# Weight slots 8256 bytes apart and moving rows at four byte offsets, in a two-layer decoder trunk

## The reference

```python
for i in range(DEPTH):                       # DEPTH = 2
    g = norm_gains[i]
    y = swiglu(rms_norm(h, g[0]), ffn_w_gate[i, 0], ffn_w_up[i, 0], ffn_w_down[i, 0])
    h = h + 0.5 * rms_norm(y, g[1])
    u = rms_norm(h, g[2])
    y = mixer_ab(u, ...) if i % 2 == 0 else mixer_cd(u, ...)
    h = h + rms_norm(y, g[3])
    y = swiglu(rms_norm(h, g[4]), ffn_w_gate[i, 1], ffn_w_up[i, 1], ffn_w_down[i, 1])
    h = h + 0.5 * rms_norm(y, g[5])
return h[:, N_META:]

def swiglu(x, w_gate, w_up, w_down):         # 1024 -> 2816 -> 1024
    return (jax.nn.silu(x @ w_gate) * (x @ w_up)) @ w_down
```

## Time and profile before

| what | value |
|---|---|
| median of the runs shown | 1092.51 us (1092.21 to 1092.80) |
| the profiled execution | 1092.85 us, span 1091.1 us |
| granted TensorE clock, mean | 0.998 |
| busy: TensorE, VectorE, ScalarE | 1077.3, 703.8, 545.5 us |
| DMA engines, mean | 54.1% on the weight queue |

### The profile page before, as it was taken

The page is one execution under the profiler, slowest core; times in us unless marked ns, Lnnn a source line. Parts: engine busy times, 40 slices in busy tenths (PEclk is TensorE's granted clock), DMA queues, the critical chain, the costliest instruction groups (busy, mean ns, idle before and its releaser), DMA issues.

```text
span 1091.1 us, 19370 instructions
## 1 busy us (share of the span) xinstructions
PE 1077.3 (99%) x8599; PEld 1046.3 (96%) x8599; DVE 703.8 (65%) x770; ACT 545.5 (50%) x635; POOL 1.6 (0%) x13
## 2 busy tenths in 40 slices
PE   9999999999999999999999999999999999999997
PEld 8999999999999999999999999999999899999986
DVE  6856654588996777655546755654568867665552
ACT  5644343467564765343544644343475766444431
POOL 0000000000000000000000000000000000000000
PEclk9999999999999999999999999999999999999999
DMA  9666556857751545564554655555553244666451
GB/s 315 194 193 184 179 174 167 163 112 182 156 163 39 155 155 171 177 192 148 178 180 127 219 180 168 183 173 178 162 179 117 78 155 156 192 193 206 143 173 39
DMA packets 173072, 180.02 MB, mean 165 GB/s; under 512 B 7508, under 2 KB 165804, under 8 KB 172988
## 3 DMA queue, kind: packets, MB, share of 16 engines
q1 hardware_dynamic: 172668, 177.66, 54.1%
q10 hardware_dynamic: 320, 1.11, 0.3%
HBM read 177.05 MB, written 1.71 MB: 164 GB/s over the span
## 4 chain that ended last, share of the span: by engine, by line
PE 88%; DVE 7%; ACT 2%; DMA 2%; issue 1%; SPq 0%; ACTq 0%; DVEq 0%
PE ps L1800 23%; PE ps L1801 23%; PE ps L1802 23%; PE ps L1905 5%; PE ps L1890 2%; PE ps L1889 2%; PE ps L1888 2%; PE ps L2030 2%; PE ps L1872 2%; PE ps L1834 1%; PE ps L1837 1%; PE ps L1838 1%; DVE w_lo L1179 1%; DVE hT L1228 1%; DMA a_dram<-dN 1%
## 5 line engine op out<-in xcount | busy, mean ns | idle before, releaser
L1800 PE MATMUL ps<-u,w_hi 128*128 128x272 f32 (+1 forms) x1648 | 473.6, 287 | 2.1 <-DVE w_lo L1179 1.8
L1801 PE MATMUL ps<-u,w_hi 128*128 128x272 f32 (+1 forms) x1648 | 470.0, 285 | 0.0
L1802 PE MATMUL ps<-u,w_lo 128*128 128x272 f32 (+1 forms) x1648 | 469.7, 285 | 0.0
L1179 DVE TENSOR_TENSOR w_lo<-raw,w_hi 128x2048 fp32r<-128x2048 f32 (+2 forms) x167 | 369.5, 2236 | 106.0 <-ACT w_hi L717 106.0
L717 ACT ACTIVATE w_hi<-raw 128x2048 fp32r<-128x2048 f32 (+2 forms) x167 | 310.8, 1871 | 162.2 <-PE ps L1802 140.0
L1800 PEld LDWEIGHTS ps<-u,w_hi 128*128 128x128 f32 x1648 | 310.4, 188 | 4.2 <-ACT yT L846 1.4
L1801 PEld LDWEIGHTS ps<-u,w_hi 128*128 128x128 f32 x1648 | 310.4, 188 | 0.3
L1802 PEld LDWEIGHTS ps<-u,w_lo 128*128 128x128 f32 x1648 | 310.1, 188 | 0.0
L1800 PE MATMUL ps<-hid,w_hi 128*128 128x272 f32 x528 | 151.3, 286 | 0.0
L1801 PE MATMUL ps<-hid,w_hi 128*128 128x272 f32 x528 | 151.3, 286 | 0.0
L1802 PE MATMUL ps<-hid,w_lo 128*128 128x272 f32 x528 | 151.3, 286 | 0.0
(11 more groups left out here) (345 smaller groups left out, 1045.2 us busy)
## 6 DMA issues: line engine op xcount, KB each, us to landing
raw<-ffn_w_up SPq DMA_DIRECT2D x44, 1024.0 KB, 5.4
raw<-ffn_w_gate SPq DMA_DIRECT2D x43, 1024.0 KB, 5.3
raw<-ffn_w_down SPq DMA_DIRECT2D x24, 896.0 KB, 4.9
raw<-ffn_w_down SPq DMA_DIRECT2D x20, 1024.0 KB, 5.1
raw<-ab_w_in SPq DMA_DIRECT2D x16, 1024.0 KB, 14.6
raw<-cd_w_in SPq DMA_DIRECT2D x9, 1024.0 KB, 5.5
raw<-ab_w_out SPq DMA_DIRECT2D x4, 1024.0 KB, 7.0
raw<-cd_w_out SPq DMA_DIRECT2D x4, 1024.0 KB, 5.1
```

The source lines that it names most:

```text
L1179: dve.tensor_tensor(dst, src, w_hi[:, n % NW, 0:rows(n) * CB].bitcast(F32), ALU.subtract)\
L1800: pe.matmul(o, wh, rhs_hi[:, kk, tok], start=first and kk == 0, stop=False)
L1801: pe.matmul(o, wh, rhs_lo[:, kk, tok], start=False, stop=False)
L1802: ins = pe.matmul(o, wl, rhs_hi[:, kk, tok], start=False, stop=last and kk == rows(n) - 1)
```

## The change

The slots of raw, w_lo and w_hi get 16 floats more and so lie 8256 bytes apart. The place of u_room and of hidden becomes 0 modulo 256 instead of 64, and the shifts of the sublayers get four values. gains moves from the spare floats of the rows to a place of its own, and lnv from a place of its own to a part of the scratch memory. No instruction is added, removed or moved on any engine; the operands' addresses change.

```diff
@@ -48,9 +48,10 @@
 BANK = 512
 ROW = 320
 SPARE = 288
-PLACE = 64
-U_AT = (0, 0, 0, 0, 0, 64)
-HID_AT = (0, 0, 0, 64)
+PLACE = 0
+SLOT = RAW + 16
+U_AT = (0, 64, 128, 192, 64, 192)
+HID_AT = (64, 192, 0, 0)
@@ -172,11 +173,13 @@
         ring = place[0]
-        raw = sb("raw", [NR, RAW])
-        w_lo = at("w_lo", [P, NR, RAW], F32R, ring)
-        w_hi = sb("w_hi", [NW, RAW], F32R)
+        raw = sb("raw", [NR, SLOT])
+        w_lo = at("w_lo", [P, NR, SLOT], F32R, ring)
+        w_hi = sb("w_hi", [NW, SLOT], F32R)
         ss = sb("ss", [T])
         rstd = sb("rstd", [2, T])
+        gains = sb("gains", [3, 4 * KD])
+        place[0] += (PLACE - place[0]) % 256
         u_place = place[0]
@@ -191,10 +194,9 @@
-        lnv = sb("lnv", [T])
         ident = sb("ident", [P])
         ones = sb("ones", [P])
-        w_ba, gains = spare[:, 0:KD, :], spare[:, KD:KD + 3, :]
+        w_ba = spare[:, 0:KD, :]
@@ -207,6 +209,7 @@
         y_sq = at("y_sq", [P, 2, 2, T], F32, scratch)
+        lnv = at("lnv", [P, T], F32, scratch + (HG + 1) * TP * 4)
@@ -1728,7 +1731,7 @@
-            dve.tensor_copy(gains, ps[:, 0, 0:12 * KD].rearrange("p (r c) -> p r c", c=32)).then_inc(s_gains, 1)
+            dve.tensor_copy(gains[:, :, :], ps[:, 0, 0:12 * KD].rearrange("p (r c) -> p r c", c=32)).then_inc(s_gains, 1)
```

## The result

The changed kernel took 1105.16 us, the median of 1103.45 and 1106.87, against 1092.51: ratio 1.011, 95% interval 1.0082 to 1.0138. It is slower by 12.7 us. The forecast was 1106.5.

A forecast was written before the change was run, and what follows sets the result against it. TensorE was taken as the bound, its matmul spacing set by byte distances. Terms 12.7 + 1.2 - 0.2 + 0.9 + 0.3 - 0.8 = +14.1 us on the 1092.51 median gave 1106.5 us; range 1097 to 1113, main case's own 1103 to 1112.

The forecast's parts named there:

- What bounds the kernel: Whole kernel: TensorE, busy 1077.3 of 1091.1 us, is the bound; its waits for w_lo should stay under 3 us.
- The distance decides, not the place: TensorE matmuls: the moving row's byte distance from the weights, not its own address, sets the time between matmul starts.
- Even distances slow, odd ones fast: 272-column matmuls: distances 0 or 128 modulo 256 take 127.5 ns, distances 64 or 192 take 123.3 ns.
- The price: 272-column matmuls in FFNs, mixers and output projection: half of 6048 get 4.2 ns slower, +12.7 us.
- The last FFN: Input matmuls of the last sublayer's FFN, 256 columns: 528 get 2.2 ns slower, +1.2 us.
- The last down projection: Last sublayer, weights streaming 512 columns: half of 264 matmuls go from 233.3 to 240 ns, +0.9 us.
- Cover in the mixers: Mixer sublayers: a third of 2.5 us of slower matmuls hides behind VectorE and ScalarE work, -0.8 us.
- Passings between blocks: TensorE between weight blocks: some 65 passings from slow to fast rows cost a few ns each, +0.3 us.
- rival 5: Half of the blocks: w_hi and w_lo 128 apart change distance twice per matmul triple, +12 us, 1118.5 us; chance 0.07.
- rival 4: Half of the blocks: weights away from 128 shed part of the extra 10 ns, 118.3 ns, 1077.5 us; chance 0.06.
- rival 3: All matmuls: addresses don't matter in the long run, time stays 1092.5 us; chance 0.08.
- rival 2: All matmuls: only an even weight start together with an even moving-row start is slow, 1099.5 us; chance 0.12.

## Why the prediction was right

Forecast 1106.5, measured 1105.16, inside the range 1097 to 1113 and inside the case's own 1103 to 1112. By stages the sum of 14.1 us stands against 10.5 in the profiled execution: the three FFNs cost 1 us more than forecast, the mixers and the last sublayer 4.2 less. That the total lands 1.3 us off is in part luck. By its steps:

- *What bounds the kernel*: right. TensorE's busy time grew by 11.7 us and the span by 10.5; the other engines' busy times and the landing stayed, and the waits for w_lo fell from 1.8 to 0.8 us, under the 3 us that the prediction set as its sign.
- *The distance decides, not the place*: right, shown by shifting everything (ratio 0.9996) and by equal distances at different places in the changed kernel (blocks 9 and 92).
- *Even distances slow, odd ones fast*: wrong. Distance 192 is slow, 126.7 ns, shown by the kernel with that distance throughout. The step failed because I took the odd row 192 in the earlier trace rows for a steady state: its three matmuls stand between two slow rows and their sum, 0.37 us, is not what 24 of them do. The stretch with 256 columns at 192 was steady, but 256 columns follow another table (117.8 at 192, 120.0 at 0), and I carried it over.
- *The price*: 4.2 ns for half of 6048 against 2.1, 3.3 and 3.3 ns for three quarters; 2.1 and 2.2 ns on the mean. Two errors, a class missed and a price too high, cancelled; that is luck. With one distance per sublayer the same step would have been far off: it gives 0 for distance 192, where the run had 3.3 ns a matmul.
- *The last FFN*: +1.2 forecast, -0.1 measured. Its blocks have 120.0 ns at worst, but block 147, for one, has 113.3 for its 48 matmuls, with w_hi at distance 192 and w_lo at 64; no row before had shown such a spacing. *The last down projection*: +0.9 forecast, -0.8 measured: the earlier trace rows were the slowest of the three distances that a run shows pure, not a fast one: 233.3 ns at 192, 228.9 at 64, 226.7 at 0. So even my argument for "distance decides" rested on a wrong reading of 233.3 ns, though its conclusion held.
- *Cover in the mixers*: a third of 2.5 us forecast as hidden. 768 input matmuls of sublayer 1 at 125.2 instead of 123.5 ns make 1.3 us, and the stage took the same time in both profiles (174.08 and 174.03). But with its inputs at distance 64 it took 173.1 to 173.3 us in seven other profiles and 174.9 in one, so the profile before was 0.8 us above the usual, and the true cover lies somewhere between 0.5 us and all of it. In sublayer 4 0.5 us showed.
- *Passings between blocks* (+0.3): no run shows them apart from the rest.
- *Much slower, by w_hi and w_lo lying apart* (rival 5): refuted, such blocks lie between the classes (124.4 to 126.2 ns). *Faster* (rival 4): not at 272 columns, no block is under 123.3. *No effect* (rival 3): refuted by 123.3 to 126.7 ns for the same instruction by the addresses alone. The Trainium skill, "TensorE: Matmul & The Clock Gate", says in step 1 of Part 2 that the two read ports are independent and that loading the next weights takes no read bandwidth from the running matmul, and in "Wait — 56ns, not 53.3ns?" that matmuls back to back start N / 2.4 + 2.5 ns apart; for 272 columns that is an estimate of 115.8 ns. No run here has it: 123.3 is the smallest at 272 columns. Nor do the two streams behave as independent: moving one of them by 128 bytes took a matmul from 123.3 to 126.7 ns, moving both by 64 bytes changed nothing.
- The 1099.5 us of rival 2 are 1099.2 by its own terms.

The median of the changed kernel is from two executions 3.4 us apart; the profiled one is the lower, and what made the other longer is not shown.

## What to carry to other kernels

Where TensorE streams fp32r back to back with a weight load for each matmul, the distance between the two start addresses modulo 256 was worth up to 3% of a matmul at 272 and 512 columns and up to 6% at 256, so fix one for all blocks and measure the few candidates; spreading blocks over several offsets buys the mean of good and bad ones. A spacing read from a few matmuls between others is no steady one: take it from a stretch of at least one block. Price each length of the moving operand by its own rows: distance 80 was as good as 64 at 272 columns and worse at 256, and at 512 columns distance 0 was the best of three.

## What the runs showed of the hardware that I had not expected

- The spacing depends on weights minus row: at 272 columns 123.3 ns for 64 to 96 bytes, 124.4 for 16 and 112, 125.4 for 0, 126.6 for 32, 48, 128 and 192; at 256 columns 120.0 for 0 and 160, 118.7 for 128, 117.8 for 192, 119.3 for 80, 117.3 for 96, and 113.3 or 117.8 for 64; at 512 columns, hidden rows stationary, 226.7 for equal places and 228.9 or 233.3 for 64 and 192. The medians of ScalarE's split (1903 ns) and VectorE's (2285), and of the landing (5.3 us), did not feel their offsets.
- 256 columns at distance 64 have two rhythms, 113.3 and 117.8 ns, that hold for more than 100 us; one switch came with a short wait, another in mid-stream, and executions of one program seem to differ by it, 1084.9 against 1089.6 us. I know of no edit that makes the fast one certain. With 272 columns one rhythm a distance was all that I saw.
- The mechanism, which reads of the two streams meet and where, was not measured and stays open. The price of a mixture isn't the mean of its parts (128/64/128 at 126.7, 192/64/192 at 124.4), and growing distances (125.4) differ from falling ones (124.5).
